# Third layer's scan: segment sums and diagonal product side by side, with one run of ten projection matmuls for a head

## The chip, the cores and the metric

The program runs on one core of a Trainium2 chip. Its time is the device time of one execution in microseconds; for the kernel before it was taken three times. A profile of one further execution shows what each engine did: TensorE (PE, its weight loads apart as PEld), VectorE (DVE), ScalarE (ACT), GpSimd (POOL) and the DMA queue of SyncE (SP).

## The reference

Three transformer layers over 512 tokens of width 1024, in float32. The first two are attention layers. The third is a hybrid: one input projection feeds a state-space branch (a scan over 16 heads of 64 columns) and a stick-breaking attention branch. The change lies in the scan of the state-space branch:

```
proj = einsum('bld,de->ble', rmsnorm(x), w_in)
z_ssd, xbc, dt_raw, q, k, v, z_sb, gates = split(proj)
...
seg    = a_cs[..., :, None] - a_cs[..., None, :]
decay  = exp(where(causal, seg, -inf))
scores = einsum('bclgn,bcsgn->bgcls', cc, bc)
attn   = scores[:, :, None] * decay
y_diag = einsum('bgrcls,bcsgrp->bclgrp', attn, x_dt)
...
y = y_diag + y_off + xh * d_skip
```

`seg`, `decay`, `attn` and `y_diag` exist once for each of the 16 heads. The kernel computes them in 4 blocks of 128 tokens, all four blocks of a head in one instruction where it can. Beside this it computes other columns of the same input projection (part of `z_ssd`, and `v`), on which the scan doesn't depend.

## The kernel before

Every projection is done in three products: activations and weights are split into a high and a low part, and high x high, high x low and low x high are added up in PSUM. A *piece* is a weight tile of up to 128x1024 values. SyncE loads it into `w_raw` (4 buffers), ScalarE rounds it to `w_hi` (L512), GpSimd subtracts to get `w_lo` (L527). There are two buffers of `w_hi` and `w_lo`, so piece q+2 is rounded once the matmuls of piece q are done, and its `w_lo` is made after that.

**The scan, head by head.** Four PSUM banks belong to the scan (`OB`, `OB+1` for the segment sums, `OB+2`, `OB+3` for the diagonal products, each taken in turn), four to the projection beside it (`ZB+g`, one for each block g of 128 tokens). For head n:

- TensorE: one bf16 matmul of 80 rows and 512 columns, the segment sums (L1727).
- ScalarE: `Relu` out of the bank into `att[n % 2]` (L1606), then `Exp` in place (L1608).
- VectorE: `att` times the masked scores (L1857, both inputs in SBUF).
- TensorE: the diagonal product, 4 matmuls of 64 columns in float32 (L1739), which the trace shows as 8.
- VectorE: the result plus the skip term into `c_y` (L1863), and after heads 3, 7 and 11 a product of 1024 columns (L1872).

TensorE takes the diagonal product of head n-1 in iteration n. Its waits are `ssd_att` (the VectorE product of that head is there) and `ssd_y` (the bank is free).

**The projection beside it.** `pC_z` is 16 pieces q of 24 matmuls, x = 24q to 24q+23, in 4 groups of columns c = q // 4. The four pieces of a group fill the four banks `ZB+g`; in a piece the first six matmuls go to block 0, the next six to block 1, and so on. Group 0 is 256 columns wide, the others 512. Matmuls x = 0 to 63 stand beside the transposes before the scan. The list `BESIDE` says how many follow in each *slot*; in the scan there are two slots to an iteration. When a slot holds the last matmul of a piece, ScalarE does that piece's work in the place of that slot in its own program: at the end of a group it copies the four banks out (L1668), and then it rounds piece q+2 (L512). ScalarE's program is a fixed order; in iteration n it is `Relu` n, `Exp` n, then what the slots of iteration n hold. The first matmul of a new group into bank `ZB+g` waits for the copy of that bank (L1646).

GpSimd's `w_lo` instructions and SyncE's loads follow the pieces in their order, whatever the slots are.

After the heads come 12 matmuls for the states and their use (L1750, L1759), with 6 projection matmuls behind each, and one last slot with the rest of the 384.

Of the kernel before, what the change touches and what calls it, by code (L numbers as in the profile page):

```python
# [30 lines left out]
MB = T // P  # L31
# [14 lines left out]
C_H, C_G, C_N, TAPS = 16, 2, 128, 4  # L46
# [154 lines left out]
def reached(k, n, least):  # L201


    return not isinstance(k, int) or k > 0 or n >= least
# [16 lines left out]
def build(nc, i, out):  # L221
    ctx = ExitStack()
    with ctx:
# [1320 lines left out]
        XT = 2 * MB + C_G  # L1544
# [4 lines left out]
        def ssd_act(act):  # L1549
            S = pC_x  # L1550

            def silu(k, n):
                act.wait_ge(sem["conv_acc"], n + 1 + 4 * k)
                nc.scalar.activation(xcT[:, ds(4 * k + n, 1), :].rearrange("p o t -> p (o t)"),
                                     acc[n % 2], ACT.Silu).then_inc(sem["conv_out"], 1)

            def take(k, s, g):
                n = s * S.groups + g
                if reached(k, n, 2):
                    act.wait_ge(sem["conv_acc"], n - 1 + 4 * k)  # L1560
                nc.scalar.activation(x_in[n % 2][:, TAPS - 1:TAPS - 1 + T], bank_of(S, s, g)[:, :],
                                     ACT.Copy).then_inc(S.evac.sem, 1)
                if reached(k, n, 1):
                    silu(k, n - 1)
            project_act(act, pC_zd, split=3)
            nc.scalar.activation(a_neg[:, :], alog_row, ACT.Exp).then_inc(sem["ssd_ready"], 1)
            act.wait_ge(sem["ssd_dt"], 1)
            nc.scalar.activation(acs, acs, ACT.Exp).then_inc(sem["ssd_ready"], 1)
            act.wait_ge(sem["ssd_ready"], 2)
            nc.scalar.activation(acs, acs, ACT.Ln, bias=one_t[:, :]).then_inc(sem["ssd_ready"], 1)  # L1570
            nc.scalar.activation(done_t[:, :], one_t[:, :], ACT.Silu)

            def choose():
                act.wait_ge(sem["chosen_made"], 1)
                nc.scalar.activation(seg_key[0:HD], chosen[0:HD, 0:C_H].unsqueeze(2).to_broadcast([HD, C_H, P]),
                                     ACT.Copy).then_inc(sem["seg_in"], 1)
                nc.scalar.activation(seg_query[HD:SEG_ROWS],
                                     chosen[HD:SEG_ROWS, C_H:C_H + MB].unsqueeze(2).to_broadcast([4 * MB, MB, P]),
                                     ACT.Copy).then_inc(sem["seg_in"], 1)

            def collect_parts():
                for n, b in enumerate(SEG_BANKS):
                    act.wait_ge(sem["parts_turned"], n + 1)
                    if n == 0:
                        nc.scalar.activation(seg_query[0:HD].rearrange("p m l -> p (m l)"), bank[b][0:HD, :],
                                             ACT.Copy).then_inc(sem["seg_in"], 1)
                    nc.scalar.activation(seg_key[HD:SEG_ROWS, 4 * n:4 * n + 4].rearrange("p h s -> p (h s)"),
                                         bank[b][HD:SEG_ROWS, :], ACT.Copy).then_inc(sem["seg_in"], 1)
            project_act(act, S, take, after=(choose, collect_parts))
            for f in range(XT):  # L1590
                if f == 5:
                    silu(S.n // 2 - 1, 3)
                act.wait_ge(sem["xT_turned"], f + 1)
                to = c_x[:, f // 2, f % 2 * 512:f % 2 * 512 + 512] if f < 2 * MB else \
                    c_B[:, f - 2 * MB].rearrange("p m n -> p (m n)")
                nc.scalar.activation(to, bank[OB + (f + 2) % 4][:, :], ACT.Copy).then_inc(sem["xT_out"], 1)
                beside_act(act, f)
            act.wait_ge(sem["acs_parted"], 1)
            nc.scalar.activation(acs_sums, acs_sums, ACT.Exp).then_inc(sem["ssd_ready"], 1)
            for n in range(C_H + 1):  # L1600
                if n < C_H:
                    act.wait_ge(sem["ssd_seg"], n + 1)
                    if n >= 2:
                        act.wait_ge(sem["ssd_diag"], n - 1)
                    fall = att[n % 2].rearrange("p m l -> p (m l)")
                    nc.scalar.activation(fall, bank[OB + n % 2][:, :], ACT.Relu).then_inc(sem["ssd_fall"], 1)  # L1606
                    act.wait_ge(sem["ssd_fall"], n + 1)
                    nc.scalar.activation(fall, fall, ACT.Exp, scale=-1.0).then_inc(sem["ssd_exp"], 1)  # L1608
                beside_act(act, XT + 2 * n)
                beside_act(act, XT + 2 * n + 1)  # L1610
            for n in range(LAST_SLOT - XT - 2 * (C_H + 1)):
                beside_act(act, XT + 2 * (C_H + 1) + n)
                if n < 2 * MB:
                    if n == 0:
                        act.wait_ge(*pC_z.evac(2 * MB))
                    z = (z_right[:, n // 2], z_left[n // 2])[n % 2]
                    nc.scalar.activation(z, z, ACT.Silu).then_inc(sem["z_silu"], 1)
            project_act(act, pC_zs, between=lambda m: store_rows(act, m))
# [8 lines left out]
        def turn_bank(m, a):  # L1627
            return bank_of(pC_zs, m, 2 + a)

        BESIDE = [6] * (2 * MB) + [8] * C_G + [9, 9, 9, 5] + [5, 5] * (C_H - 1) + [6] * (4 * (MB - 1))  # L1630
        BESIDE.append(4 * 4 * 24 - sum(BESIDE))
        LAST_SLOT = len(BESIDE)

        def ended(slot):
            before = sum(BESIDE[:slot])
            return range(before // 24, (before + BESIDE[slot]) // 24)

        def beside_pe(pe, slot):
            before = sum(BESIDE[:slot])
            for x in range(before, before + BESIDE[slot]):  # L1640
                q, g, kk, t = x // 24, x // 6 % 4, x // 3 % 2, x % 3
# [14 lines left out]
        def beside_act(act, slot):  # L1656
            for q in ended(slot):
                c = q // 4
                if q % 4 == 3:
                    if c == 1:  # L1660
                        act.wait_ge(sem["ssd_y"], C_H // 2)
                    if c == 2:
                        act.wait_ge(sem["ssd_diag"], C_H)
                        act.wait_ge(sem["ssd_ready"], 4 + MB - 1)
                    for g in range(MB):
                        act.wait_ge(C["product"].sem, pC_z.done_after(0, q, g))
                        to = (z_left[g][:, ZW:512], z_right[:, g], s_v[:, g, 0:512], s_v[:, g, 512:1024])[c]
                        nc.scalar.activation(to, bank[ZB + g][:, 0:to.shape[1]],  # L1668
                                             ACT.Copy).then_inc(pC_z.evac.sem, 1)
                split_ahead_act(act, pC_z, 0, q)  # L1670
                for m in range(2 * (q - 13), 2 * (q - 13) + 2) if q in (13, 14) else ():
                    norm_act_step(act, ssd_norm, m, lambda m: (sem["ssd_gated"], 2 * m + 2), rounds=False)
# [6 lines left out]
        def ssd_pe(pe):  # L1679
# [43 lines left out]
            for n in range(C_H + 1):  # L1723
                if n < C_H:
                    if n >= 2:
                        pe.wait_ge(sem["ssd_fall"], n - 1)
                    nc.tensor.matmul(bank[OB + n % 2][:, :], seg_key[0:SEG_ROWS, n],  # L1727
                                     seg_query[0:SEG_ROWS].rearrange("p m l -> p (m l)"),
                                     start=True, stop=True).then_inc(sem["ssd_seg"], 1)
                beside_pe(pe, XT + 2 * n)  # L1730
                if n:
                    a = n - 1
                    pe.wait_ge(sem["ssd_att"], n)
                    if a >= 2:
                        pe.wait_ge(sem["ssd_y"], a - 1)
                    else:
                        pe.wait_ge(sem["ssd_sc_out"], C_G)
                    for m in range(MB):
                        mm = nc.tensor.matmul(bank[OB + 2 + a % 2][:, m * HD:(m + 1) * HD], att[a % 2][:, m, :],  # L1739
                                              c_xdt[:, m, a * HD:(a + 1) * HD], start=True, stop=True)  # L1740
                    mm.then_inc(sem["ssd_diag"], 1)
                beside_pe(pe, XT + 2 * n + 1)
            slot = XT + 2 * (C_H + 1)
            pe.wait_ge(sem["ssd_ready"], 4 + MB - 1)
            pe.wait_ge(sem["ssd_y"], C_H)
            for n in range(2 * (MB - 1)):
# [429 lines left out]
        n = pieces[pC_zd.piece0][0] * pieces[pC_zd.piece0][1]  # L2176
# [288 lines left out]
```

## Time and profile before

| | |
|---|---|
| median of 3 runs | 1193.01 us (1192.43 to 1193.63) |
| the profiled execution | 1192.82 us, span 1191.1 us |
| PE busy | 1174.2 us (99%), 6127 matmuls |
| PEld busy | 913.0 us (77%) |
| ACT, DVE, POOL busy | 594.0, 535.5, 427.8 us |
| granted TensorE clock | 0.999 of full speed |
| the iterations of the heads | 664.9 to 721.4 us of the span |

The share of busy time is over the whole span. Starts and durations of matmuls overlap in the records, since they are pipelined: the distance from one start to the next tells what one costs, not its duration. A row of the chain gives such distances.

### The profile page before, as it was taken

To read this page: it belongs to the slowest core of one execution; us is meant where nothing else is said; L and a number is where in the kernel's file an instruction comes from. 1 tells how busy PE (TensorE), PEld (TensorE's weight loads), DVE (VectorE), ACT (ScalarE), POOL (GpSimd) and SP (SyncE) were. 2 spreads that over 40 slices of the span, in tenths; PEclk is the share of its full clock that TensorE was granted. 3 is DMA by queue.
4 is the path that set the end of the run, shared out by engine and by line. 5 is a ranking of instruction groups with operands and counts; after the bars stand their busy time and mean duration, and the time that the engine had idled before them with its cause. 6 is when DMAs were issued, how large, how long until landed. Compare 5 with 4: busy or idle time off the path is not lost.

```text
span 1191.1 us, 16234 instructions
## 1 busy us (share of the span) xinstructions
PE 1174.2 (99%) x6127; PEld 913.0 (77%) x6127; DVE 535.5 (45%) x981; ACT 594.0 (50%) x1246; POOL 427.8 (36%) x259
## 2 busy tenths in 40 slices
PE   8999999999999999999999999999999999999998
PEld 7988855568988666668888987887666677888886
DVE  4311465545210655454466546512777750033333
ACT  7354666655352655574545654534655552243142
POOL 6534721124344222314343332444222223444451
PEclk9999999999999999999999999999999999999999
DMA  8433211113336999812321312233221112232321
GB/s 300 142 106 69 65 23 47 54 54 84 98 103 69 96 62 93 123 39 74 107 89 53 123 55 71 74 89 104 70 55 54 54 54 89 89 106 89 103 92 71
DMA packets 111549, 100.97 MB, mean 85 GB/s; under 512 B 21156, under 2 KB 98288, under 8 KB 111472
## 3 DMA queue, kind: packets, MB, share of 16 engines
q1 hardware_dynamic: 108928, 95.35, 34.1%
q0 software_dynamic: 864, 3.15, 0.7%
q10 hardware_dynamic: 1680, 1.44, 0.4%
q8 instruction: 49, 0.80, 0.3%
q14 instruction: 28, 0.23, 0.1%
HBM read 94.68 MB, written 2.10 MB: 81 GB/s over the span
## 4 chain that ended last, share of the span: by engine, by line
PE 89%; DMA 6%; ACT 2%; DVE 1%; issue 1%; POOL 1%; SPq 0%; DVEq 0%; ACTq 0%
PE bank L606 49%; PE bank L1957 8%; PE bank L1650 7%; DMA w_raw<-in_w_in_b 3%; PE bank L1442 3%; PE bank L877 3%; PE bank L895 2%; PE bank L911 2%; PE bank L1973 2%; DMA w_raw<-in_w_out 2%; PE bank L1267 2%; PE bank L1988 2%; PE bank L2000 2%; PE bank L881 1%; PE bank L1739 1%; DMA w_raw<-in_w_mem_kv 1%
## 5 line engine op out<-in xcount | busy, mean ns | idle before, releaser
L527 POOL TENSOR_TENSOR w_lo<-w_raw,w_hi 128x1024 fp32r<-128x1024 f32 (+4 forms) x157 | 355.1, 2262 | 689.8 <-ACT w_hi L512 689.7
L512 ACT ACTIVATE w_hi<-w_raw 128x1024 fp32r<-128x1024 f32 (+6 forms) x161 | 159.2, 990 | 232.2 <-PE bank L606 202.8
L606 PE MATMUL bank<-acts_hi,w_hi 128*128 128x512 f32 (+1 forms) x576 | 224.0, 389 | 1.0 <-POOL w_lo L527 1.0
L606 PE MATMUL bank<-acts_lo,w_hi 128*128 128x512 f32 (+1 forms) x576 | 222.5, 386 | 0.0
L606 PE MATMUL bank<-acts_hi,w_lo 128*128 128x512 f32 (+1 forms) x576 | 222.5, 386 | 0.0
L606 PEld LDWEIGHTS bank<-acts_hi,w_hi 128*128 128x128 f32 x576 | 108.2, 188 | 24.4 <-POOL w_lo L527 1.5
L606 PEld LDWEIGHTS bank<-acts_lo,w_hi 128*128 128x128 f32 x576 | 108.2, 188 | 22.1
L606 PEld LDWEIGHTS bank<-acts_hi,w_lo 128*128 128x128 f32 x576 | 108.2, 188 | 21.3
L2094 DVE TENSOR_TENSOR_SCAN arena_end<-arena 128x512 f32<-128x512 f32 (+3 forms) x64 | 83.8, 1310 | 60.3 <-ACT arena L2045 60.3
L606 PE MATMUL bank<-w_hi,acts_hi 128*128 128x512 f32 (+4 forms) x240 | 87.0, 362 | 0.2 <-POOL w_lo L527 0.2
L606 PE MATMUL bank<-w_hi,acts_lo 128*128 128x512 f32 (+4 forms) x240 | 86.2, 359 | 0.0
L606 PE MATMUL bank<-w_lo,acts_hi 128*128 128x512 f32 (+4 forms) x240 | 86.0, 358 | 0.0
L606 PE MATMUL bank<-w_more,acts_hi 128*128 128x512 f32 (+3 forms) x296 | 75.4, 341 | 0.0
L993 DVE TENSOR_REDUCE stat<-bank 128x1 f32<-128x256 f32 (+3 forms) x80 | 34.0, 459 | 83.7 <-PE bank L877 51.0
L1002 DVE TENSOR_SCALAR arena<-arena,stat 128x256 f32<-128x256 f32 (+3 forms) x128 | 68.8, 537 | 4.6
L527 POOL TENSOR_TENSOR w_more<-w_raw,w_more 128x1024 fp32r<-128x1024 f32 (+4 forms) x21 | 43.5, 2090 | 40.7 <-ACT w_more L512 40.7
L1957 PE MATMUL bank<-acts_hi,w_hi 128*128 128x512 f32 x144 | 58.0, 402 | 0.1
L1957 PE MATMUL bank<-acts_hi,w_lo 128*128 128x512 f32 x144 | 57.5, 399 | 0.0
L951 ACT ACTIVATE arena<-bank,stat 128x256 f32<-128x256 f32 (+3 forms) x80 | 39.9, 504 | 33.2 <-DVE stat L993 33.1
L1957 PE MATMUL bank<-acts_lo,w_hi 128*128 128x512 f32 x144 | 56.3, 391 | 0.0
L606 PEld LDWEIGHTS bank<-w_more,acts_hi 128*128 128x128 f32 x296 | 51.5, 188 | 3.8
L962 ACT ACTIVATE arena<-bank 128x256 f32<-128x256 f32 (+3 forms) x128 | 47.0, 420 | 14.6 <-PE bank L911 12.4
(302 smaller groups left out, 2114.2 us busy)
## 6 DMA issues: line engine op xcount, KB each, us to landing
w_raw<-in_w_in SPq DMA_DIRECT2D x64, 512.0 KB, 3.6
w_raw<-in_w_out SPq DMA_DIRECT2D x24, 512.0 KB, 3.6
w_raw<-in_w_in_b SPq DMA_DIRECT2D x22, 512.0 KB, 5.2
w_raw<-in_w_in_a SPq DMA_DIRECT2D x10, 512.0 KB, 4.1
w_raw<-in_w_mem_kv SPq DMA_DIRECT2D x8, 512.0 KB, 8.2
w_raw<-in_w_sb_proj SPq DMA_DIRECT2D x8, 512.0 KB, 3.4
w_raw<-in_w_ssd_proj SPq DMA_DIRECT2D x8, 512.0 KB, 3.5
arena_shared<-junk SPq DMA_DIRECT2D x11, 256.0 KB, 20.6
```

Of the source, the lines that this page charges most:

```text
L512: nc.scalar.activation(w_at(p)[0][:, 0:size], w_raw[p % RAW][:, 0:size], ACT.Copy).then_inc(w_high.sem, 1)
L527: nc.gpsimd.tensor_tensor(lo[:, 0:size], w_raw[p % RAW][:, 0:size], hi[:, 0:size].bitcast(F32), ALU.subtract).then_inc(w_rest.sem, 1)
L606: mm = nc.tensor.matmul(bank_of(S, s, g)[0:lhs.shape[1], 0:rhs.shape[1]], lhs, rhs, start=j + kk + t == 0, stop=j == len(S.pieces) - 1 and ...
L877: mm = nc.tensor.matmul(bank[2 + (2 * s + e) % 4][:, 0:n], X.q(e)[:, b * P:(b + 1) * P], X.k(e)[:, 0:n], start=True, stop=not X.causal)
L951: nc.scalar.activation(w2[i % 4][:, 0:n], src[:, 0:n], ACT.Exp, bias=stat[:, i % 8:i % 8 + 1], scale=-1.0 if X.less else 1.0, accum_out=st ...
L962: nc.scalar.activation(wT2[e][:, 0:blocks, b * P:(b + 1) * P], bank[6 + i % 2][:, 0:blocks * P].rearrange("p (c t) -> p c t", c=blocks), A ...
L993: nc.vector.tensor_reduce(stat[:, i % 8:i % 8 + 1], bank[2 + i % 4][:, 0:n], AX.X, ALU.max, negate=True).then_inc(A.lowest.sem, 1)
L1002: nc.vector.tensor_scalar(w2[i % 4][:, 0:n], w2[i % 4][:, 0:n], stat[:, 16 + i % 8:17 + i % 8], None, ALU.mult).then_inc(A.weights.sem, 1)
L1442: mm = nc.tensor.matmul(bank[0][:, :], w[:, kk * P:(kk + 1) * P], acts[:, kk, :], start=x == 0, stop=x == 23)
L1650: mm = nc.tensor.matmul(bank[ZB + g][:, 0:n], x_[:, 2 * j + kk, g * P:(g + 1) * P], w[:, kk * n:kk * n + n], start=j + kk + t == 0, stop=j ...
L1957: mm = nc.tensor.matmul(qk_bank(q)[:, :], w[:, kk * P:(kk + 1) * P], acts[:, kk, :], start=x == 0, stop=x == 23)
L2094: nc.vector.tensor_tensor_scan(left[i % 2][:, T - n:T][:, ::-1], x, x, 1.0, ALU.mult, ALU.bypass).then_inc(sem["scan"], 1)
```

## The change

In the iterations of the heads the two slots become one. TensorE's order in iteration n is now segment sums of head n, diagonal product of head n-1, and then the slot's projection matmuls. Slots of this part were 9, 9, 9, 5 and then 5, 5 for each iteration; they are now 16, 14 and then 10 for each iteration from n = 2 on. That makes 180 projection matmuls in this part instead of 182, and the last slot takes 68 instead of 66. ScalarE's program follows the new slots.

```diff
--- before.py
+++ after.py
@@ ssd_act
                     nc.scalar.activation(fall, fall, ACT.Exp, scale=-1.0).then_inc(sem["ssd_exp"], 1)
-                beside_act(act, XT + 2 * n)
-                beside_act(act, XT + 2 * n + 1)
-            for n in range(LAST_SLOT - XT - 2 * (C_H + 1)):
-                beside_act(act, XT + 2 * (C_H + 1) + n)
+                beside_act(act, XT + n)
+            for n in range(LAST_SLOT - XT - (C_H + 1)):
+                beside_act(act, XT + (C_H + 1) + n)
@@
-        BESIDE = [6] * (2 * MB) + [8] * C_G + [9, 9, 9, 5] + [5, 5] * (C_H - 1) + [6] * (4 * (MB - 1))
+        BESIDE = [6] * (2 * MB) + [8] * C_G + [16, 14] + [10] * (C_H - 1) + [6] * (4 * (MB - 1))
@@ ssd_pe
                                      start=True, stop=True).then_inc(sem["ssd_seg"], 1)
-                beside_pe(pe, XT + 2 * n)
                 if n:
                     a = n - 1
                     pe.wait_ge(sem["ssd_att"], n)
@@
                     mm.then_inc(sem["ssd_diag"], 1)
-                beside_pe(pe, XT + 2 * n + 1)
-            slot = XT + 2 * (C_H + 1)
+                beside_pe(pe, XT + n)
+            slot = XT + C_H + 1
```

## Rows read from the trace of the kernel before

**Rows 1.** The page: busy time by engine, and the chain by engine.
```profile
PE 1174.2 (99%) x6127; PEld 913.0 (77%) x6127; DVE 535.5 (45%) x981; ACT 594.0 (50%) x1246; POOL 427.8 (36%) x259
...
PE 89%; DMA 6%; ACT 2%; DVE 1%; issue 1%; POOL 1%; SPq 0%; DVEq 0%; ACTq 0%
```

**Rows 2.** The chain that ended last, 660 to 765 us: start, length, what.
```profile
673.70 0.23 PE bank L1727
673.94 1.16 PE bank L1650 x5
675.09 0.84 PE bank L1739 x8
675.93 1.21 PE bank L1650 x5
677.14 0.23 PE bank L1727
...
717.20 2.35 PE bank L1650 x10
```

**Rows 3.** Busy time by stretch: the stretch, then engine by engine, clock, DMA.
```profile
676.99:680.43 3.44, 3.44 (x21) 2.80 (x21) 1.77 (x3) 2.18 (x3) 0.73 (x1) 1.00 0.04 11
...
664.94:721.45 56.51, 56.51 (x329) 47.13 (x327) 27.76 (x37) 31.30 (x49) 17.69 (x8) 1.00 0.23 71
```

**Rows 4.** Timeline of PE: start, length, engine, line, what.
```profile
664.94 0.38 PE L1727 MATMUL bank<-seg_words 80*128 80x512 bf16 x1
...
667.20 0.28 PE L1650 MATMUL bank<-w_hi,acts_hi 128*128 128x256 f32 x1
667.32 0.39 PE L1727 MATMUL bank<-seg_words 80*128 80x512 bf16 x1
...
711.14 0.39 PE L1650 MATMUL bank<-w_hi,acts_lo 128*128 128x512 f32 x1
711.37 0.39 PE L1727 MATMUL bank<-seg_words 80*128 80x512 bf16 x1
```

**Rows 5.** Timeline of ACT, the same columns.
```profile
665.36 0.60 ACT L1606 ACTIVATE arena_end<-bank 128x512 f32<-128x512 f32 x1 [0.68 <-PE bank L1727]
666.00 0.63 ACT L1608 ACTIVATE arena_end<-arena_end 128x512 f32<-128x512 f32 x1
666.53 1.04 ACT L512 ACTIVATE w_hi<-w_raw 128x1024 fp32r<-128x1024 f32 x1
...
669.44 0.39 ACT L1668 ACTIVATE row<-bank 128x256 f32<-128x256 f32 x1
...
702.66 2.04 ACT L1668 ACTIVATE arena<-bank 128x512 f32<-128x512 f32 x4
704.57 1.08 ACT L512 ACTIVATE w_hi<-w_raw 128x1024 fp32r<-128x1024 f32 x1
...
711.57 1.06 ACT L512 ACTIVATE w_hi<-w_raw 128x1024 fp32r<-128x1024 f32 x1 [1.94 <-PE bank L1650]
712.53 0.58 ACT L1606 ACTIVATE arena_end<-bank 128x512 f32<-128x512 f32 x1
...
728.37 1.06 ACT L512 ACTIVATE w_hi<-w_raw 128x1024 fp32r<-128x1024 f32 x1 [5.48 <-PE bank L1650]
```

**Rows 6.** Timeline of DVE, the same columns.
```profile
666.73 0.69 DVE L1857 TENSOR_TENSOR arena_end<-arena_end,arena_shared 128x512 f32<-128x512 f32 x1 [0.89 <-ACT arena_end L1608]
669.04 1.55 DVE L1857 TENSOR_TENSOR arena_end<-arena_end,arena_shared 128x512 f32<-128x512 f32 x1 [1.62 <-ACT arena_end L1608]
...
713.80 1.83 DVE L1857 TENSOR_TENSOR arena_end<-arena_end,arena_shared 128x512 f32<-128x512 f32 x1 [2.96 <-ACT arena_end L1608]
```

**Rows 7.** Timeline of POOL, the same columns.
```profile
667.65 2.39 POOL L527 TENSOR_TENSOR w_lo<-w_raw,w_hi 128x1024 fp32r<-128x1024 f32 x1 [4.78 <-ACT w_hi L512]
...
712.71 2.38 POOL L527 TENSOR_TENSOR w_lo<-w_raw,w_hi 128x1024 fp32r<-128x1024 f32 x1 [4.59 <-ACT w_hi L512]
```

**Rows 8.** Timeline of PEld around one segment matmul.
```profile
673.54 0.10 PEld L1727 LDWEIGHTS bank<-seg_words 80*128 80x128 bf16 x1 [0.27 <-issue]
673.55 0.20 PEld L1650 LDWEIGHTS bank<-w_lo,acts_hi 128*128 128x128 f32 x1
```

**Rows 9.** Timeline at 568 to 571 us: TensorE released by VectorE.
```profile
568.34 1.66 DVE L736 SCALAR_TENSOR_TENSOR hn<-h,norm_stat,arena 128x1024 f32<-128x1024 f32 x1
...
570.04 0.86 PEld L716 LDWEIGHTS bank<-ident,hn 128*128 128x128 f32 x8 [0.56 <-DVE hn L736]
570.05 1.09 PE L716 MATMUL bank<-ident,hn 128*128 128x128 f32 x8 [0.34 <-DVE hn L736]
```

**Rows 10.** The diagonal product's line: ns min, median, max.
```profile
L1739 PEld LDWEIGHTS bank<-arena,arena_end x128: 187/192/192, 668.5 to 720.1; 128*128 128x128 f32 x128
```

## The prediction

> **What bounds the kernel now.** I read the page first. TensorE is busy for 99% of the span and holds 89% of the chain that ended last [rows 1], so a change counts only if it alters what TensorE streams or makes it wait. Next I asked for the heads' part by stretches. TensorE is busy for all 56.51 us of it at a granted clock of 1.00, the upper level of 2.4 GHz. A head's period is 3.44 us; ScalarE uses 2.18 us of the one shown, VectorE 1.77, GpSimd 0.73 [rows 3]. They are off the chain, but each lies between TensorE's segment matmul and its diagonal product, so I read their timelines for how late a result may get.
>
> The chain gives the price of a period: segment sums 0.23, five projection matmuls 1.16, diagonal product 0.84, five more 1.21, together 3.44 us [rows 2]. One projection matmul of 512 columns is 0.23 us, one of 256 columns 0.12 (667.20 to 667.32) [rows 2, 4].
>
> **What the change removes and adds.** No instruction is removed: 34 slots become 17, and 2 matmuls go from this part to the last slot, 0.46 us less here and 0.46 more there. The loads of SyncE and the subtractions of GpSimd keep their order, each still following its piece. What can be gained on TensorE is one change of kind less in a head: segment sums to projection and projection to diagonal product become one step. The chain shows ten projection matmuls in one run as 2.35 us and as two fives as 1.16 + 1.21 = 2.37 [rows 2]. I take 0.02 us for each of 15 heads, **0.3 us gained**. Bounds: nothing, and 0.06 for each (2 x 1.21 less 2.35 is 0.07), 0.9 us.
>
> **What the change makes late.** Let t be the start of head n's segment matmul. Before, its diagonal product came one period, one segment matmul and five projection matmuls later, at t + 3.44 + 0.23 + 1.16 = t + 4.83. Now it comes straight behind the next segment matmul, **at t + 3.67**. TensorE starts some 0.05 us after VectorE has ended (570.00 and 570.05) [rows 9], so the VectorE product must end by t + 3.62.
>
> The undisturbed way is short: `Relu` starts at t + 0.42 (664.94, 665.36), `Exp` 0.64 later, the product at 666.73, t + 1.79, and it ends at t + 2.48 [rows 4 to 6]. That leaves 1.1 us of slack, and most heads cost nothing.
>
> The disturbed way is long. When a piece is rounded just ahead of `Relu`, the following holds in the rows: rounding starts at 711.57, `Relu` at 712.53, 0.96 later; GpSimd starts its subtraction at 712.71 and ends at 715.09; the VectorE product starts at 713.80, inside it, takes 1.83 us instead of 0.69 and ends at 715.63, 0.54 behind GpSimd [rows 5 to 7]. So **the product ends 4.06 us after the rounding began**. The product of the second head shows the same end: 670.59, against GpSimd's 670.04 [rows 6, 7]. With s for the start of the rounding that precedes `Relu` n, the diagonal product waits if s + 4.06 is past t + 3.62, that is if s is later than t - 0.44. Before, the limit was t + 0.72 (4.83 - 0.05 - 4.06), and no wait arose.
>
> The Trainium skill (GPSIMD Engine Reference, Key points) says that GpSimd shares its SBUF interfaces with VectorE and contends with VectorE instructions that have two SBUF inputs; the 1.83 us agree. Without that contention the product would end 0.96 + 1.27 + 0.69 = 2.92 us after the rounding began, the stalls of heads 1, 7 and 12 below would be gone, the copy's would be 0.67, and the sum would be +0.5 us, 1193.5.
>
> Rounding starts 0.43 us after the start of the piece's last matmul (711.14, 711.57), and the last matmul of a slot starts 0.23 before the next segment matmul (711.14, 711.37) [rows 4, 5]. So s depends on the place j (0 to 9) of the piece's last matmul in its ten: s = t - 0.23 - 0.23 (9 - j) + 0.43. The new slots begin with x = 94 + 10 (n - 2). That gives:
>
> - q = 4, x = 119: iteration 4, j = 5, s = t - 0.72: slack 0.28.
> - q = 5, x = 143: iteration 6, **j = 9**, s = t + 0.20. The product of head 7 ends at t + 4.26; **stall 0.64 us**.
> - q = 6, x = 167: iteration 9, j = 3: slack 0.7 or more.
> - q = 7, x = 191: iteration 11, **j = 7**. This piece ends a group, so four copies stand before the rounding; four take 1.91 us (702.66 to 704.57), 0.48 each [rows 5]. The last waits for x = 191 and starts at t - 0.26, the rounding at t + 0.22. **Stall 0.66 us** in front of the diagonal product of head 12.
> - q = 8 and 9, x = 215 and 239: j = 1 and 5. The first is harmless, behind the second no head follows.
>
> **The first three heads.** The second segment matmul comes 2 matmuls of 0.12 us earlier, at 667.08, the first diagonal product is due at 667.31. Its VectorE product ends at 667.42 [rows 6]: with 0.05 for the release, **stall 0.16**. Diagonal product 0.89 us (0.84 and 0.05 for the slower five behind it), 14 matmuls of 0.12: the third segment matmul starts at 670.04, the next diagonal product is due at 670.27. Its VectorE product meets GpSimd's 667.65 to 670.04 and ends at 670.59 as before [rows 6, 7]: **stall 0.37**, and the product runs 670.64 to 671.53. Then come x = 94 and 95, and x = 96, first of a new group, is due at 671.77. It waits for the copy of its bank. Before, that copy stood ahead of `Relu` 2; now the piece's slot is that of iteration 2, so `Relu` 2 (670.46), `Exp` 2 (671.10) and only then, 0.53 later, the copy of 0.39 [rows 5] stand in front: it ends at 672.02, **stall 0.30**. The next group's copies stand at x = 192, which comes behind eight matmuls of its slot: due at t + 2.97, the copy is done by t + 2.3. No stall.
>
> **Sum.** 0.16 + 0.37 + 0.30 + 0.64 + 0.66 = 2.13 us of stalls, less 0.3 gained: **+1.8 us**. Behind a stalled matmul wait the ten projection matmuls and the next segment matmul; nobody makes the time up, since TensorE is the bound to the end. The moved slots of the last part cost nothing: ScalarE has 5.48 us of idle time ahead of one rounding there [rows 5], and TensorE covers one extra `Silu` ahead of a copy. The profiled execution is 1192.82 us, 1.7 of it outside its span of 1191.1, and would become 1194.6. The median of the runs is 0.2 above it: **1194.8 us**, +0.15%.
>
> What no row shows is what the restart of a diagonal product costs whose weights weren't loaded ahead. Rows 9 show none beyond 0.05 us; at most the load of 0.19 [rows 10] stands open five times, 0.95 us. I take nothing, by the nearer row.
>
> **The rivals.**
>
> *The pair itself costs (slower).* The segment matmul's bf16 weights are not loaded ahead: their load starts 0.27 us after the one before it ended, with the matmul itself [rows 8]. If the diagonal product's first load can't be pulled in front of that matmul's end either, up to 0.19 us [rows 10] stands open in 15 heads: 2.8 us more, 1197.6; half of it gives 1196.2. It decides from 0.04 us for each head, since 1.8 + 0.6 passes 0.2%. Against it: the projection's load behind the segment matmul starts at 673.55, with it [rows 8], and I see no reason why another float32 load should not. Chance 0.14. The five restarts at 0.95 us lead to the same side, 1195.8; with the rest of the uncertainty of the forecast they count below.
>
> *The stalls don't come (no change, or a trace faster).* If GpSimd's subtraction or ScalarE's copies fall otherwise than I worked out, the two large stalls vanish (-1.3) or all do: 1192.1 to 1193.5. For it: a start later by 0.6 us would decide. Against it: 4.06 repeats in the rows, and the places j follow from the code. Chance 0.14.
>
> *A change of kind on TensorE drains it (a gain that outweighs the stalls).* A matmul of 512 columns is recorded as 0.39 us and its successor starts after 0.23 [rows 4], so a drain would cost 0.16. One less in each of 15 heads would be 2.4 us; with 2.13 of stalls, 1192.7. Against it: the four changes in a period cost together 3.44 - 2.3 - 1.07 = 0.07 us. The Trainium skill (TensorEngine Tiling (Array Packing), Tiling Modes, Key Properties) says that changing the tiling mode drains TensorE. By that rule this would be the result only if the 80-row matmul were another mode; the trace doesn't agree. Chance 0.03.
>
> **How the numbers follow.** The forecast has the remaining 0.69; 1194.8 is its time. About 0.2% of the time, 2.4 us, is what a measurement of this kernel can tell from no change. The forecast's own range is 1193.9 (0.9 gained on changes of kind, smaller early stalls) to 1195.8 (0.95 for restarts); a quarter of it lies above 1195.4. Slower: 0.17 + 0.14 = 0.31. Faster needs the drain's gain without the stalls, 1190.6, or something unseen: 0.04. The rest, 0.65, is within 0.2%. The range for 8 in 10 takes in the second rival's upper part and half of the first rival: 1192.9 to 1196.6.
>
> **What would show it.** In the profile after: periods of 3.42 us without a wait in most heads; TensorE waiting for VectorE at L1739 four times, the longest at heads 7 and 12 with some 0.65 us each; one wait of L1650 for ScalarE's copy, 0.3 us; VectorE products of 1.83 us that end 4.06 us after a rounding began. Wrong would be: periods longer than 3.44 in undisturbed heads (first rival), no waits at heads 7 and 12 (second), periods below 3.38 (third).

## The result and the profile after

The changed kernel takes 1195.32 us (median of 18 runs, 1194.55 to 1196.16); the kernel before took 1192.55 us (18 runs) beside it. The ratio is 1.0022, with a 95% interval of 1.0016 to 1.0028: **2.6 us slower** by the ratio (1.9 to 3.3), 2.8 us by the two medians. That is clear of no change, but the interval takes in the 0.2% that was named as the limit of what can be told. The forecast was 1194.8 us, +1.8 us, in a range of 1192.9 to 1196.6.

The profiled execution of the changed kernel took 1195.8 us with a span of 1194.1. Where the time lies is told first by the waits, in the heads' part (waiting line, releaser: us in total, times, longest). The diagonal product is now L1737, the segment matmul L1726, the projection L1649, VectorE's product L1855, ScalarE's copy L1667.

```profile
PEld bank L1737 <- DVE arena_end L1855: 2.4, 4, 0.8
...
PE bank L1649 <- ACT arena_end L1667: 0.2, 1, 0.2
```

TensorE waits for VectorE four times and for a copy once; before, nothing released it in this part but its own queue. The 2.4 us count from the end of the last weight load, so they hold time in which TensorE still streamed the segment sums; what a wait costs is read further down, from when a matmul was due and when it starts. The same in the busy time by stretch, from the first segment matmul to the first state matmul:

```profile
665.49:724.03 58.54, 57.16 (x327) 46.77 (x325) 26.63 (x37) 30.32 (x48) 16.69 (x7) 1.00 0.22 69
```

This stretch was 56.51 us [rows 3] and holds 2 projection matmuls less now, 0.46 us: 58.54 - (56.51 - 0.46) = **2.49 us more**, so most of the 2.6 to 2.8 us arises in this part. (One execution differs from another by itself: ahead of the heads, where the programs are the same, the two profiled ones are 0.55 us apart, 664.94 and 665.49.) The granted clock is 1.00 as before.

The chain of work that ended last shows an undisturbed period and a disturbed one (start, length, what):

```profile
681.71 0.23 PE bank L1726
681.94 0.84 PE bank L1737 x8
682.78 2.35 PE bank L1649 x10
...
688.60 0.02 ACT w_hi L512
688.62 0.94 issue
689.56 0.59 ACT arena_end L1606
690.15 0.02 issue
690.17 0.64 ACT arena_end L1608
690.81 0.02 issue
690.84 1.85 DVE arena_end L1855
692.68 0.04 issue
692.73 1.10 PE bank L1737 x8
```

The undisturbed period is 0.23 + 0.84 + 2.35 = 3.42 us against 3.44 [rows 2]. In the disturbed one the chain leaves TensorE and runs through ScalarE's rounding (L512), `Relu`, `Exp` and VectorE's product of 1.85 us. The timelines of ScalarE, VectorE, GpSimd and TensorE around head 7 say why:

```profile
688.60 1.06 ACT L512 ACTIVATE w_hi<-w_raw 128x1024 fp32r<-128x1024 f32 x1 [1.94 <-PE bank L1649]
689.56 0.58 ACT L1606 ACTIVATE arena_end<-bank 128x512 f32<-128x512 f32 x1
...
690.84 1.83 DVE L1855 TENSOR_TENSOR arena_end<-arena_end,arena_shared 128x512 f32<-128x512 f32 x1 [3.06 <-ACT arena_end L1608]
...
689.73 2.40 POOL L527 TENSOR_TENSOR w_lo<-w_raw,w_hi 128x1024 fp32r<-128x1024 f32 x1 [5.37 <-ACT w_hi L512]
...
688.40 0.39 PE L1726 MATMUL bank<-seg_words 80*128 80x512 bf16 x1
...
691.83 0.39 PE L1726 MATMUL bank<-seg_words 80*128 80x512 bf16 x1
692.73 1.10 PE L1737 MATMUL bank<-arena,arena_end 128*128 128x64 f32 x8 [0.51 <-DVE arena_end L1855]
693.64 0.48 PE L1649 MATMUL bank<-w_lo,acts_hi 128*128 128x512 f32 x1
```

The rounding of a piece starts at 688.60, 0.20 behind head 7's segment matmul (688.40), so `Relu` comes at 689.56. GpSimd's subtraction runs from 689.73 to 692.13, the product that starts inside it ends at 692.67, 4.07 us after the rounding began and 0.54 behind GpSimd. The diagonal product was due 0.23 behind the segment matmul of 691.83, at 692.06. It starts at 692.73, a wait of 0.67 us. Then it occupies TensorE for 0.91 us until the next projection matmul (693.64).

The reader should compare this 0.91 with an undisturbed head, where it is 0.81:

```profile
681.55 1.09 PEld L1737 LDWEIGHTS bank<-arena,arena_end 128*128 128x128 f32 x8
...
681.78 1.00 PE L1737 MATMUL bank<-arena,arena_end 128*128 128x64 f32 x8
682.59 0.48 PE L1649 MATMUL bank<-w_lo,acts_hi 128*128 128x512 f32 x1
```

Here the first weight load starts at 681.55, with the segment matmul, 0.23 us ahead of its own matmul. Behind the wait at head 7 the load starts with its matmul (the view ends at 693 us, so it counts 3 of the 8 loads):

```profile
692.73 0.41 PEld L1737 LDWEIGHTS bank<-arena,arena_end 128*128 128x128 f32 x3 [0.81 <-DVE arena_end L1855]
```

The restart costs 0.10 us beyond the wait. That this is the part of the load that can't be hidden fits the rows; no run separates it from another cost of a restart.

The three waits of the opening, in the timeline of TensorE:

```profile
667.63 0.39 PE L1726 MATMUL bank<-seg_words 80*128 80x512 bf16 x1
668.02 1.10 PE L1737 MATMUL bank<-arena,arena_end 128*128 128x64 f32 x8
...
670.69 0.39 PE L1726 MATMUL bank<-seg_words 80*128 80x512 bf16 x1
671.19 1.10 PE L1737 MATMUL bank<-arena,arena_end 128*128 128x64 f32 x8
...
672.31 0.28 PE L1649 MATMUL bank<-w_hi,acts_lo 128*128 128x256 f32 x1
672.80 0.47 PE L1649 MATMUL bank<-w_hi,acts_hi 128*128 128x512 f32 x1 [0.21 <-ACT arena_end L1667]
```

A diagonal product is due 0.23 us behind its segment matmul, a projection matmul 0.12 us behind one of 256 columns. The waits are thus 668.02 - 667.86 = 0.16, 671.19 - 670.92 = 0.27 and 672.80 - 672.43 = 0.37 us. At head 12 the segment matmul in front starts at 709.75, and the diagonal product at 710.69 instead of 709.98: 0.71 us.

### The profile page after: what moved, and what is told of

Its sections match the earlier page's. It is cut to its first block, busy times and chain, and to the rows that moved or that the text cites. A ratio compares the mean times of both kernels' runs of the same rounds, so it can differ in the third digit from the quotient of the medians.

```text
span 1194.1 us, 16234 instructions
## 1 busy us (share of the span) xinstructions
PE 1175.7 (98%) x6127; PEld 913.1 (76%) x6127; DVE 532.2 (45%) x981; ACT 594.0 (50%) x1246; POOL 427.8 (36%) x259
## 4 chain that ended last, share of the span: by engine, by line
PE 88%; DMA 6%; ACT 2%; DVE 2%; issue 1%; POOL 1%; SPq 0%; DVEq 0%; ACTq 0%
PE bank L606 49%; PE bank L1955 8%; PE bank L1649 6%; DMA w_raw<-in_w_in_b 3%; PE bank L1442 3%; PE bank L877 3%; PE bank L895 2%; PE bank L911 2%; PE bank L1971 2%; DMA w_raw<-in_w_out 2%; PE bank L1267 2%; PE bank L1986 2%; PE bank L1998 2%; PE bank L881 1%; PE bank L1737 1%; DMA w_raw<-in_w_mem_kv 1%
## 5 line engine op out<-in xcount | busy, mean ns | idle before, releaser
L512 ACT ACTIVATE w_hi<-w_raw 128x1024 fp32r<-128x1024 f32 (+6 forms) x161 | 159.3, 990 | 234.4 <-PE bank L606 202.8
```

Source lines behind the costliest of these rows:

```text
L512: nc.scalar.activation(w_at(p)[0][:, 0:size], w_raw[p % RAW][:, 0:size], ACT.Copy).then_inc(w_high.sem, 1)
```

## The experiments

All kernels were built from the changed one. Where a ratio is given, the kernel before was timed beside them on the same chip; three of the experiments share its 27 runs. In the cuts of code, `@@` marks where lines are left out. Stretches are again from the first segment matmul to the first state matmul.

**Rounding after `Exp`.** ScalarE's rounding behind pieces 5 and 7 moves behind the next head's `Exp`; TensorE's program stays.

```diff
+        AFTER_EXP = (5, 7)
@@ beside_act
-                split_ahead_act(act, pC_z, 0, q)
+                if q not in AFTER_EXP:
+                    split_ahead_act(act, pC_z, 0, q)
@@ ssd_act, behind Exp n
+                    for q in ended(XT + n - 1) if n else ():
+                        if q in AFTER_EXP:
+                            split_ahead_act(act, pC_z, 0, q)
```

> The changed kernel, with ScalarE's rounding behind pieces q = 5 and 7 placed after Exp of the next head instead of ahead of its Relu; TensorE's order is untouched. Theory (a rounding ahead of Relu makes the VectorE product of heads 7 and 12 late): the iterations 8 and 13, 4.22 and 4.23 us long with the wait, fall back to 3.43, together 1.6 us less; time about 1193.7 where the changed kernel has 1195.3, ratio to the kernel before 1.0009. Rival (the pair of segment sums and diagonal product costs by itself): both waits may go, but the time stays within 0.5 us of 1195.3. Rival (GpSimd's subtraction alone makes the product late, wherever the rounding stands): the waits stay, or move to other heads.

Measured: 1193.2 us (11 runs) against 1192.65 (27 runs), ratio 1.0007 (0.9998 to 1.0016), where 1193.7 was expected. The stretch of the heads falls from 58.54 to 56.95 us:

```profile
665.05:722.00 56.95, 56.63 (x326) 46.78 (x324) 25.33 (x37) 30.45 (x48) 17.75 (x7) 1.00 0.24 72
```

That is 1.59 us less, as expected, and both waits are gone: the segment matmuls of heads 8 and 9 start at 691.40 and 694.83, 3.43 apart. The product of head 7 is over before the subtraction starts, at 690.69:

```profile
689.69 0.69 DVE L1860 TENSOR_TENSOR arena_end<-arena_end,arena_shared 128x512 f32<-128x512 f32 x1 [2.34 <-ACT arena_end L1608]
```

The pair of segment sums and diagonal product stayed as it was, so it isn't what these 1.6 us are spent on. The subtraction still runs for both pieces, and no head waits for it, so it isn't enough by itself either. The one for piece 7 now falls on head 8, whose product takes 1.58 us (693.12 to 694.70), but that head's diagonal product is due only at 695.05.

**A short subtraction.** Here the rounding stays ahead of `Relu`, and GpSimd's part is cut from 1024 to 16 columns. The kernel leaves out the rest of the low part of weight pieces 7 and 9, so it serves to measure and not to use.

```diff
-                rest(pC_z.piece0 + q + 2, piece_size(pC_z, 0, q + 2))
+                rest(pC_z.piece0 + q + 2, 16 if q in (5, 7) else piece_size(pC_z, 0, q + 2))
```

> The changed kernel with GpSimd's subtraction behind pieces q = 5 and 7 cut from 1024 to 16 columns; what is left out is w_lo of pieces 7 and 9 of this projection, apart from 16 columns. Roundings stay where they are, so Relu of heads 7 and 12 is as late as before. Theory (Relu's delay alone is harmless, the product is late because it waits for the subtraction to end): the product takes 0.69 us and ends 2.9 us after the rounding began instead of 4.07, the waits at heads 7 and 12 go, 1.6 us less, ratio 1.0009. Rival (the late Relu is enough): the waits stay at 0.8 us each, ratio 1.0022.

Measured: 1193.62 us (11 runs) against 1192.65, ratio 1.0008 (0.9999 to 1.0017); the stretch is 56.96 us, again 1.58 less.

```profile
664.23:721.19 56.96, 56.64 (x327) 46.80 (x325) 24.42 (x37) 30.32 (x48) 12.35 (x7) 1.00 0.24 71
```

ScalarE, VectorE and GpSimd around head 7:

```profile
687.35 1.06 ACT L512 ACTIVATE w_hi<-w_raw 128x1024 fp32r<-128x1024 f32 x1 [1.93 <-PE bank L1649]
688.32 0.58 ACT L1606 ACTIVATE arena_end<-bank 128x512 f32<-128x512 f32 x1
...
689.59 0.69 DVE L1855 TENSOR_TENSOR arena_end<-arena_end,arena_shared 128x512 f32<-128x512 f32 x1 [3.05 <-ACT arena_end L1608]
...
688.49 0.22 POOL L527 TENSOR_TENSOR w_lo<-w_raw,w_hi 128x16 fp32r<-128x16 f32 x1 [5.38 <-ACT w_hi L512]
```

The segment matmul of head 7 starts at 687.16 here, so `Relu` is as late as in the changed kernel (1.16 us behind it in both), but the product takes 0.69 us and ends at 690.28, 2.93 after the rounding began instead of 4.07. The two runs together show that the waits at heads 7 and 12 need both: a rounding ahead of `Relu`, and the subtraction that follows it and holds up VectorE.

**The end of piece 5 moved by two matmuls.** The last matmul of piece 5 is now the eighth of its ten and no longer the last, so its rounding starts two matmuls earlier against the segment matmul of head 7.

```diff
-[16, 14] + [10] * (C_H - 1)
+[16, 14] + [10, 10, 10, 12, 10, 10, 8] + [10] * (C_H - 8)
```

> The changed kernel with the slot of iteration 5 at 12 matmuls and that of iteration 8 at 8, so that piece q = 5 ends with the 8th of its ten matmuls (j = 7) instead of the last (j = 9), and nothing else moves behind iteration 8. Theory (the wait follows the place of the piece's end one to one): the rounding starts 0.46 us earlier against the segment matmul of head 7, and the wait in front of that head's diagonal product falls from 0.8 us (with the slower start behind it) to 0.35; the other waits stay. Rival (a wait of fixed size, or one by chance): 0.8 us or none.

One execution was taken, 1194.47 us; no verdict hangs on its time, only the trace is read. The timeline of TensorE:

```profile
691.36 0.39 PE L1726 MATMUL bank<-seg_words 80*128 80x512 bf16 x1
...
691.81 1.10 PE L1737 MATMUL bank<-arena,arena_end 128*128 128x64 f32 x8
...
694.66 0.39 PE L1726 MATMUL bank<-seg_words 80*128 80x512 bf16 x1
```

This iteration has only 8 projection matmuls and takes 3.30 us. Undisturbed it would be 3.43 - 0.46 = 2.97, so 0.33 us are lost. In the changed kernel the same iteration took 4.22 us (691.83 to 696.05), 0.79 more than 3.43. The loss follows the place of the piece's end one to one, as expected (0.35). The diagonal product starts 0.22 us after it was due, and again 0.10 us come on top.

**Only the opening mended.** The three waits of the opening are taken away, the two later ones left. With first slots of 18, 16 and 6, piece 3 ends in iteration 1, so the copies of its group stand ahead of `Relu` 2; its rounding moves behind `Exp` 2.

```diff
-[16, 14] + [10] * (C_H - 1)
+[18, 16, 6] + [10] * (C_H - 2)
@@ with the edit of the first experiment
+        AFTER_EXP = (3,)
```

> The changed kernel with the first slots 18, 16, 6 instead of 16, 14, 10 and the rounding behind q = 3 after Exp of head 2; the roundings behind q = 5 and 7 stay ahead of Relu. Theory (the losses add up wait by wait): the three waits of the opening are gone, the two at heads 7 and 12 stay at 0.79 us of period each; time 0.9 us below the changed kernel, 1.4 us above the kernel before, ratio 1.0012. Rival (TensorE's waits overlap with something that bounds the part anyway): the time of the changed kernel, 1.0022, or that of the kernel before.

Measured: 1194.45 us (11 runs) against 1192.42 (15 runs), ratio 1.0013 (1.0004 to 1.0022). The stretch is 57.56 us, 0.98 less than in the changed kernel; of TensorE's waits for another engine only the two large ones are left (second view: waiting line, releaser, us in total, times, longest):

```profile
665.07:722.63 57.56, 56.51 (x327) 46.62 (x324) 26.80 (x37) 30.61 (x48) 16.70 (x7) 1.00 0.24 71
```
```profile
PEld bank L1742 <- DVE arena_end L1860: 1.6, 2, 0.8
```

**All waits out.** Both edits at once: first slots 18, 16, 6 and `AFTER_EXP = (3, 5, 7)`. Nothing is left out of the computation.

> The changed kernel with the first slots 18, 16, 6 instead of 16, 14, 10 (same sum) and the roundings behind pieces q = 3, 5 and 7 after Exp of the next head. Theory (five waits are the whole loss, and the pair saves about 0.015 us for each head): no wait of TensorE for VectorE or ScalarE left in the heads' part, time 0.2 us below the kernel before, ratio 0.9998; no verdict. Rival (the pair costs by itself): 1 us or more above the kernel before, without a wait in the trace. Rival (a change of kind drains TensorE): 2 us below it.

Measured: 1192.48 us (11 runs) against 1192.65 (27 runs), ratio 1.0 (0.9991 to 1.0009). No wait of TensorE for another engine is left between the first and the last head; it is busy for the whole stretch:

```profile
664.47:720.45 55.98, 55.98 (x327) 46.68 (x325) 25.49 (x37) 30.74 (x48) 17.74 (x7) 1.00 0.24 73
```

55.98 us is 2.56 less than the changed kernel's 58.54, and 0.98 + 1.59 = 2.57: the waits add up. Against the kernel before (56.51 - 0.46 = 56.05) it is 0.07 us less, which no timing of the whole can show. From head 3 to head 15 the segment matmuls of this run start at 672.71 and 713.83, 3.427 us apart on average; before they were 3.438 apart (673.55 and 714.81). Freed of its waits, the order side by side is thus worth next to nothing here; with them it costs 2.5 us.

## Why the prediction was right, step by step

| Term | forecast, us | measured, us | from |
|---|---|---|---|
| wait of diagonal product 0 | 0.16 | 0.16 | due 667.86, starts 668.02 |
| wait of diagonal product 1 | 0.37 | 0.27 | due 670.92, starts 671.19 |
| wait for the copy at x = 96 | 0.30 | 0.37 | due 672.43, starts 672.80 |
| wait at head 7 | 0.64 | 0.67 | due 692.06, starts 692.73 |
| wait at head 12 | 0.66 | 0.71 | due 709.98, starts 710.69 |
| restart behind a wait for VectorE | 0 | 4 x 0.10 | 0.91 or 0.92 against 0.81 us |
| a change of kind less | -0.3 | -0.17 | 15 x (3.438 - 3.427) |
| sum | 1.8 | 2.4 | the stretch shows 2.49 |

The place of each of the five waits, what ends it and nearly its size came out of the rows of before, and the runs confirm the mechanism: the product ends 4.07 us after the rounding began (4.06 in the forecast), 2.93 without the subtraction (2.92). The near miss came as forecast too: head 5 was given 0.28 us of slack, and its product ends at 684.91, 0.24 us before the limit of 685.15, with no wait. The five waits add up to 2.18 us, against 2.13.

The size of the change was forecast less well than the time itself. The forecast went from 1193.01 us to 1194.8; the kernel before took 1192.55 beside the changed one, 0.46 lower, and the change was +2.6 to 2.8 us and not +1.8. That the time is only 0.5 us off is in part luck. The case to which the prediction gave 0.65, a change within 0.2%, is neither confirmed nor refuted by a ratio of 1.0022 whose interval starts at 1.0016.

The two terms that were mis-sized both erred to the same side. **The restart**: the forecast kept 0 to 0.19 us each as a bound and took nothing, "by the nearer row", the transposes of [rows 9]. The measured 0.10 us is about the middle of the bound. Those rows show the start after a release, not how long TensorE is held by a first load that wasn't made ahead. **The gain**: 0.02 us for each head was read off chain pieces rounded to 0.01; over 12 heads it is 0.011. Together they are 0.5 us, and they move the sum from 0.15% of the time to 0.20%; the ratio shows 0.22%.

Two of the waits moved for reasons that the trace shows. The second is 0.10 us shorter than forecast, since the restart of the first put off the next matmuls, and with them the moment at which the second was due. The one for the copy is 0.07 us longer: the matmul starts 0.14 us behind the end of the copy, where the forecast took 0.05, the figure for a release by VectorE:

```profile
672.38 0.28 ACT arena_end L1667
672.66 0.14 issue
672.80 2.06 PE bank L1649 x8
```

Of the rivals, *the pair itself costs* is refuted: behind the segment matmul the first load of the diagonal product is pulled ahead (681.55), and with all waits out the heads' part takes 55.98 us against 56.05 before, where this rival wanted 2.8 us more. *The stalls don't come* is refuted by the trace after. *A change of kind drains TensorE* is refuted by the same 0.011 us for each head, where a drain would have given 0.16.

The reason in one sentence: TensorE's own work is the same in either order, but the diagonal product is now due 3.67 us after its segment matmul instead of 4.83, and in two of 16 heads ScalarE's and GpSimd's work for the projection makes the way through `Relu`, `Exp` and VectorE longer than that; in the opening, shorter runs and a copy moved behind `Exp` do the same.

## What to carry to other kernels

When work is grouped on the engine that bounds a kernel, list what each group does to the distance between a producer and its consumer there, and compare this with the longest way through the other engines, not the usual one. In eight of the 16 heads VectorE's product ended 2.41 us after the segment matmul, with 1.2 us to spare; 1.6 us of the loss came from the two heads in front of which a piece of other work ended. Such places can be counted from the program's order and the durations in the trace of before. The cure was to put the work that isn't urgent behind the urgent chain (rounding after `Exp`). The matmuls that use the rounded piece come 24 places later, and with all waits out none of them waited.

## What the runs showed that was not expected

- GpSimd and VectorE hold each other up in both directions. In the changed kernel seven products of VectorE start inside a subtraction, at different places in it, and take 0.70 to 1.84 us; undisturbed ones take 0.69. All seven end 0.54 or 0.55 us behind the subtraction. So the end of the subtraction sets the end of the product, and the 4.06 us of the forecast hold only where the rounding, `Relu` and the subtraction stand as close as at heads 7 and 12. The other direction: in the first experiment a subtraction started in the same moment as VectorE's product of 1024 columns (L1875 there, both inputs in SBUF) and took 3.46 us instead of 2.39, 1.07 more (3.47 in the run with all waits out); the VectorE instruction kept its 1.22 us. Both are the same place of the program, and no run varied it:

```profile
690.69 1.22 DVE L1875 TENSOR_TENSOR arena<-arena,arena_shared 128x1024 f32<-128x1024 f32 x1
...
690.69 3.46 POOL L527 TENSOR_TENSOR w_lo<-w_raw,w_hi 128x1024 fp32r<-128x1024 f32 x1 [6.76 <-ACT w_hi L512]
```

- A wait of TensorE for VectorE costs 0.10 us more than its length where a diagonal product, with its float32 weight loads, stands behind it. All four such waits of the changed kernel show it, and so does the run with the end moved, where the wait is only 0.22 us.
